# The load of a cached sequence's query rows, moved to the head of an earlier job on SyncE's queue

## The reference, cut to what matters

```python
gather = lambda c: c[l][page_table].reshape((DB, past_len) + c.shape[3:])
ka_all = jnp.concatenate([gather(cache_diff_k).astype(kas.dtype), kas], axis=1)
kf_all = jnp.concatenate([gather(cache_fox_k).astype(kfs.dtype), kfs], axis=1)
...
oa_s = _diff_attend(q1s, q2s, ka_all[..., :DA_QK_DIM], ka_all[..., DA_QK_DIM:],
                    va_all, pos_s, kpos_s, lam)
of_s = _fox_attend(qfs, kf_all, vf_all, cf_all[:, past_len:], cf_all, pos_s, kpos_s)
```

## Time and profile before

| What | Value |
|---|---|
| Median of 3 runs | 1506.2 us (1505.4 to 1510.13) |
| Time of the profiled execution | 1511.48 us |
| Its span, first to last instruction | 1509.7 us |
| PE busy | 1442.5 us, 96% of the span |
| DVE, ACT, POOL busy | 862.5, 636.9, 370.2 us |
| Mean granted TensorE clock | 0.983 |
| Query loads | 8 of 512 KB, median 4.5 us from issue to landing |
| Key page loads | 128 of 256 KB, median 2.9 and 3.1 us |
| Weight tile loads (L442) | 24 of 512 KB, median 4.6 us |

### The profile page before, as it was taken

One profiled execution on the slowest core, in us unless ns is written; L12 is line 12 of the kernel. 1 busy time (PEld: TensorE's weight loads), 2 busy tenths in 40 slices (PEclk: granted clock), 3 DMA queues, 4 the chain that ended last, 5 costly groups with the idle time before them and its releaser, 6 DMA issues. The chain is left out here.

```text
span 1509.7 us, 26823 instructions
## 1 busy us (share of the span) xinstructions
PE 1442.5 (96%) x10396; PEld 1297.5 (86%) x10396; DVE 862.5 (57%) x1378; ACT 636.9 (42%) x1194; POOL 370.2 (25%) x548
## 2 busy tenths in 40 slices
PE   7999989999998999889999999999999999999998
PEld 6999777767767677468789999999999999999998
DVE  6412566565554546465547876666776646444673
ACT  6723555544354434443332633323333324343543
POOL 5213876764654442032100000000000000000120
PEclk9999999999999999899999999999999999999999
DMA  5213546666755654622223222222222236655773
GB/s 183 56 35 92 176 153 220 213 209 227 240 174 181 199 181 124 202 85 71 71 84 93 71 77 79 85 84 85 71 85 71 71 133 207 202 187 178 235 263 112
DMA packets 174840, 209.91 MB, mean 139 GB/s; under 512 B 22051, under 2 KB 118891, under 8 KB 174676
## 3 DMA queue, kind: packets, MB, share of 16 engines
q1 hardware_dynamic: 174714, 208.21, 43.6%
HBM read 178.37 MB, written 29.88 MB: 138 GB/s over the span
## 5 line engine op out<-in xcount | busy, mean ns | idle before, releaser
L629 POOL TENSOR_TENSOR k_page<-k_page,q_bc 128x256 f32<-128x256 f32 x256 | 186.9, 762 | 130.3 <-DMA k_page<-in_cache_fox_k 102.8
L1205 PE MATMUL PS<-ht_hi,w_hi 128*128 128x344 f32 x576 | 196.5, 341 | 6.3 <-POOL w_lo L600 3.3
L1205 PE MATMUL PS<-ht_hi,w_lo 128*128 128x344 f32 x576 | 186.8, 324 | 0.0
L1205 PE MATMUL PS<-ht_lo,w_hi 128*128 128x344 f32 x576 | 186.7, 324 | 0.0
L2435 PE MATMUL PS<-act_hi,wd_hi 128*128 128x344 f32 x528 | 169.2, 321 | 2.6 <-DVE act_lo L2270 2.6
L2435 PE MATMUL PS<-act_hi,wd_lo 128*128 128x344 f32 x528 | 168.8, 320 | 0.0
L2435 PE MATMUL PS<-act_lo,wd_hi 128*128 128x344 f32 x528 | 168.6, 319 | 0.0
L838 ACT ACTIVATE probs<-probs,stat 128x256 f32<-128x256 f32 (+7 forms) x128 | 98.7, 772 | 137.6 <-DVE stat L1082 137.3
L2267 DVE TENSOR_TENSOR wd_lo<-wd_raw,wd_hi 128x1024 fp32r<-128x1024 f32 (+1 forms) x88 | 85.8, 978 | 112.2 <-ACT act_hi L2078 92.3
L1205 PEld LDWEIGHTS PS<-ht_hi,w_hi 128*128 128x128 f32 x576 | 111.3, 193 | 32.1 <-issue 25.1
L2075 ACT ACTIVATE wd_hi<-wd_raw 128x1024 fp32r<-128x1024 f32 (+1 forms) x88 | 74.2, 844 | 139.1 <-DMA act_raw<-a_dram 102.5
(11 more groups left out here) (280 smaller groups left out, 3319.5 us busy)
## 6 DMA issues: line engine op xcount, KB each, us to landing
wd_raw<-in_w_down SPq DMA_DIRECT2D x44, 512.0 KB, 3.5
k_page<-in_cache_diff_k SPq DMA_DIRECT2D x64, 256.0 KB, 2.9
k_page<-in_cache_fox_k SPq DMA_DIRECT2D x64, 256.0 KB, 3.1
v_page<-in_cache_diff_v SPq DMA_DIRECT2D x64, 256.0 KB, 2.8
v_page<-in_cache_fox_v SPq DMA_DIRECT2D x64, 256.0 KB, 3.1
w_raw<-in_w_in SPq DMA_DIRECT2D x24, 512.0 KB, 4.6
a_dram<-conv SPq DMA_DIRECT2D x22, 516.0 KB, 3.1
act_raw<-a_dram SPq DMA_DIRECT2D x66, 172.0 KB, 3.7
```

The lines of the kernel that those rows point to most:

```text
L629: ins = pool.tensor_tensor(kpage[:, g % 2, c:c + PIECE], kpage[:, g % 2, c:c + PIECE], qbc[:, c:c + PIECE], ALU.mult)
L1205: ins = pe.matmul(PS[0:rows, z_bank(c), 0:THIRD], b[:, k, :], a[:, k, third(i)], start=(k == 0 and p == 0), stop=(k == KC - 1 and p == 2))
```

## The change

The query load is put into a function of its own, and for b = 1 to 5 it is called at the head of the job in which POOL multiplies the last page of the sequence before: behind the stores of that job, ahead of its value page, its weight tile and its key page. Its wait, `mult_done` at least 8 b, is unchanged, and goes with it.

```diff
+            query_first = lambda b: k_job(PAGES * b - 3) + 1 < k_job(PAGES * b - 1)
+
+            def load_query(b):
+                sp.wait_ge(mult_done, PAGES * b)
+                sp.dma_start(qbc[:, :], io["qs_dram"][b:b + 1, :].to_broadcast([P, 2 * GRP])).then_inc(qbc_in, 16)
+
             def load_key_page(g):
...
-                if b and n == 0:
-                    sp.wait_ge(mult_done, g)
-                    sp.dma_start(qbc[:, :], io["qs_dram"][b:b + 1, :].to_broadcast([P, 2 * GRP])).then_inc(qbc_in, 16)
+                if b and n == 0 and not query_first(b):
+                    load_query(b)
...
                         sp.dma_start(od_dram[b], o_part[:, :]).then_inc(od_stored, 16)
+                for b in range(1, DB):
+                    if k_job(PAGES * b - 1) == J and query_first(b):
+                        load_query(b)
                 for g in range(DB * PAGES):
                     if (v_job(g - 2) if g >= 2 else v_job(0) - 2) == J:
                         load_value_page(g)
```

## The result

The changed kernel takes 1513.74 us in the median of 21 runs (1507.65 to 1519.88), the kernel before 1509.97 us in 21 runs on the same chips (1501.27 to 1513.61). The ratio is 1.0032, with a 95% interval of 1.0019 to 1.0044: 4.8 us slower, by 2.9 to 6.6. The medians differ by 3.8 us. The forecast was 1515.2 us, in a range that holds the result, and it gave 0.73 to slower by over 0.3%.

The account below looks back on a forecast made before the run. PE, busy in 96% of the span, was taken as the bound. Stall 4.6, slow clock 3.0 and job 3's 1.4 sum to 9.0 us, on a median of 1506.2 giving 1515.2 us, range 1508.5 to 1519.

Parts of the forecast that it names:

- The query load can't leave earlier in job 31, and all behind it leaves later: Job 31: query load still leaves at 394.30; weight tile leaves 1.94 us later, lands at 402.24, and ACT stands 7.0 us.
- PE loses 4.6 us in one stretch: Job 33: PE waits for ACT's copies behind the late tile, 7.0 less 2.4 us to spare; bounds 3.2 and 4.9.
- Jobs 10, 17 and 24 cost nothing: Key pages leave some 4 us later there, but no weight tile stands in these jobs and DVE's spare time hides it.
- Job 3 costs 1.4 us: Key page 8 lands 1.9 us later, POOL runs 1.4 us later, and PE loses that in job 7; bounds 0 and 2.6.
- there is no cover on this chain: From POOL's page 8 through page 10 and DVE to PE's wait in job 7: POOL's 1.4 us reach PE.
- The slow clock behind the stall costs 3.0 us: After PE's idle stretch, 5.9 us at 1.2 GHz, half of it lost; bounds 0 and about 3.4 us.
- The stall alone: Rival, chance 0.16: tile lands after 4.6 us, clock holds, PE loses 3 to 4 us, job 3 covered: 1509.5 us.
- The load does come early and that pays: Rival, chance 0.07: POOL begins earlier, PE's 1.89 us wait in job 7 shrinks, tile lands before ACT needs it: 1504.3 us.
- If PE were not held, DVE would stall 4 us there, and then wait for PE anyway: Late key page of job 31, done by POOL at 406.4: its lateness was taken as hidden by PE's own 4.6 us.

Follow-up runs that it names:

- wait alone: Kernel before, all loads in place, plus an SP wait at the head of job 31 for page 39 to be multiplied: 1513.93 us, 1.0021 to before.
- changed kernel again: The changed kernel run once more, unaltered, beside new runs of the kernel before: 1516.62 us, ratio 1.0042 to before.
- b = 5 alone: Changed kernel with only the fifth sequence's query load moved, in job 31; the others as before: 1512.55 us, ratio 1.0017 to before.
- Copies first: Changed kernel, but in job 33 ACT copies transposed probabilities out before rounding the weight tile: 1512.64 us, 1.0024 to before; run again 1513.76, 1.0018.
- The kernel with the four loads: Changed kernel with only the query loads of b = 1 to 4 moved, b = 5 as before: 1511.0 us, ratio 1.0009 to before.
- rounding last: Changed kernel, but in job 33 ACT rounds the weight tile behind its copies, exponentials and new rows: 1512.14 us, ratio 1.0007 to before.
- ACT's order mended everywhere: ACT rounds weight tiles behind copies and exponentials in every such job: kernel before 1503.35 us (0.9958); changed kernel, last in job 33, 1507.82 us (0.9992).

## Why the prediction was right, and where its sum was not

**The query load can't leave earlier in job 31, and all behind it leaves later: right.** The tile was forecast to leave 1.94 us behind the query load and left 1.95 behind it. ACT was to stand 7.0 us and stood 7.25 (5.72 and 6.58 in two other executions). The wait alone, on the kernel before, shows that it is the place of the wait in the queue, not the load.

From the query load's issue to ACT's start on the tile it took 8.1 us for the 1.57 MB (7.9 forecast from rows; 7.0 in the changed kernel again, 7.8 in b = 5 alone). The Trainium skill ("DMA: Bandwidth & Descriptors", Anatomy of one DMA) gives 2.0 us and the bytes over 436 GB/s for one DMA on the gpsimd path; taken for the whole burst, that is an estimate of 5.6 us. The traces disagree here too, on SP's queue.

**PE loses 4.6 us in one stretch: right.** Measured 4.74, 4.07, 3.88 and 3.21 us in four executions with this wait, all ended by ACT's a_t, 4.0 in the mean. In time the three kernels with this wait were 3.4 to 3.8 us net above before, the same within the errors. (Copies first, with a wait half as long, was no faster: see below.)

**Jobs 10, 17 and 24 cost nothing: right.** Together with job 3 they gave -0.7 ± 1.3 us net.

**Job 3 costs 1.4 us: not to be seen in the time.** The key page left at 184.54 and POOL began 2.6 us later, as the forecast has it. The 1.4 us don't come out of its own terms: 1.9 us later, less 0.26 us of idle time, less 0.6 us for a multiplication of 2.8 us in place of 3.39, are 1.0. POOL's multiplication took 3.40 us again, and POOL began its next page 2.3 us later (195.32 against 192.99). PE's wait in job 7 grew by 0.85 us only. The step that fails is "there is no cover on this chain": PE got to its wait 1.6 us later itself (204.16 against 202.55), having run at 1.2 GHz for part of 172 to 176 us (granted clock 0.58 there, 1.00 before). Over all profiled executions that wait was 0.93 to 2.74 us where job 3's loads stand as changed (seven executions, mean 2.1) and 1.22 to 2.03 where they stand as before (four, mean 1.6). The kernel with the four loads shows no cost.

**The slow clock behind the stall costs 3.0 us: the mis-sized term.** The mechanism is there. Windows of PE around the stall in b = 5 alone (length, busy, clock, DMA share, GB/s):

```profile
400.00:404.00 4.00, 0.64 (x3) 0.93 1.07 356
404.00:408.00 4.00, 4.00 (x28) 0.65 0.96 355
```

And in the wait alone:

```profile
404.00:408.00 4.00, 2.17 (x10) 0.62 0.90 281
408.00:412.00 4.00, 4.00 (x23) 0.53 1.01 393
```

The first is 4 x (0.07 + 0.35) = 1.7 us lost, the second 4 x (0.38 + 0.47) = 3.4 us; the changed kernel's two executions lost 1.7 each. So the forecast took the longer of two sizes. With PE's wait at 2 us or less in job 33 (copies first) the clock stayed at 1.00 there. The forecast's lower bound was such a case, a stretch with 1.9 us idle that kept 1.00. The kernel before has the other case too: behind job 7's wait of 1.89 us the clock fell (windows of PE before, as above):

```profile
204.00:208.00 4.00, 3.56 (x18) 0.68 0.43 119
208.00:212.00 4.00, 4.00 (x34) 0.90 0.31 115
```

And over whole runs no extra loss is seen: in the mean it was 20 to 22 us in each of the kernels with the stall and 20 to 21 in before, with errors of 1 to 3 us. Whether it is had back elsewhere isn't shown; the stretches at 1.2 GHz lie at other places in each execution.

**The sum and the base.** The sum was 9.0 us, the measured difference 3.8 (medians) to 4.8 us (ratio). That the forecast of 1515.2 came within 1.5 us of the median is luck: the base was low by nearly as much as the sum was high. The median of 3 runs was 1506.2, that of 21 is 1509.97. The forecast's chance for slower by over 0.3% rested on the whole sum; the measured ratio is just above that bound.

**Rivals.** "The stall alone" was nearest in size: a stall of 3 to 5 us and little else. Its reasons were wrong: it had the tile land after 4.6 us and the clock hold, but the tile took 6.2 and 5.1 us in the changed kernel's two executions, and the clock fell in both. "The load does come early and that pays" is out: neither with the tile saved from the wait nor from GpSimd's queue was anything gained. "If PE were not held, DVE would stall 4 us there, and then wait for PE anyway" was half right: DVE stood 4.49 us with the rounding last, and PE then waited 2.2 us for what follows from it.

**Open.** That the late tile makes ACT and then PE stand in job 33, and that issuing the tile ahead of the wait takes this and the loss away, is shown. How the whole time follows from PE's waits isn't. Copies first took 4 us off the stretch and 0 to 1 us off the time. Rounding last left 2.1 us in the stretch and 0.3 in the time. And with ACT's order mended everywhere the moved loads cost 5.0 ± 2.7 us, of which the stretch has 2.3. The profiles are one execution each, and the differences are near their errors.

## What to carry to other kernels

A load that must wait doesn't become early by being issued early on an in-order queue: it leaves at the same moment, and makes every load behind it late. Before moving one up, look at what ended the wait in front of it, then for each load that it passes at the instruction that takes its tile, and what stands behind that instruction on its engine. Here the last step was the one that cost. In the kernel before, mending it (work that nobody waits for yet goes behind copies that PE waits for) gave 0.42%, while moving the load gave nothing in any order. The two don't add up: with both, the kernel is about where it was.

## What the runs showed of the hardware

- The median time to landing hides bursts. Over the 24 weight tiles of the kernel before it is 4.6 us; behind a query load and a value page, without a pause, the tile took 5.0 to 6.3 us in seven executions, and 6.0 with the value page alone in front (the wait alone).
- The clock: PE's stall of 4.1 us before a granted clock of 0.65 in the next 4 us, one of 3.9 us before 0.62 and 0.53 in two such stretches. Shorter waits went both ways: one of 2.0 us with 1.00 throughout, one of 1.9 us with 0.68 and 0.90 behind it. In the mean over its runs every kernel lost 18 to 22 us of its 1510 to stretches at 1.2 GHz, however its stalls were placed.
- A load issued by GpSimd took 0.60 us of that engine (seven of its eight issues, 597 to 639 ns), one by SP 0.33 to 0.42 us of its queue, and landed after 4.0 to 7.8 us, against 3.5 to 5.3 us from SP in the kernel before.
